# A one-layer hybrid decoder step: the next tile's gate chain moved into the current tile, half of a projection and a broadcast moved ahead

## The chip, the cores and the metric

One NeuronCore of a Trainium2 chip runs the program. The metric is the device time of one execution in microseconds (us). TensorE is called PE here, VectorE DVE, ScalarE ACT, GpSimd POOL, and SyncE, which issues the DMAs, SP.

## What is computed

A prompt of 2048 tokens (and 8 sample tokens, one step each) goes through one layer: RMSNorm, one input projection, two attention branches side by side, gates, an output projection, a residual and a final norm.

```python
u = _rmsnorm(h, norm_g)
gla, g_gate, (sq, sk, sv), s_gate = _project(u, w_in, w_gate_up, b_gate)
o_gla, S = _gla_branch(*gla, s0, gla_norm)      # linear attention with a decay per key channel
o_swa, k_new, v_new = swa_fn(sq, sk, sv)        # 128-wide window, softmax with a sink
h = h + _merge(o_gla, g_gate, o_swa, s_gate, w_out)
```

The decay comes from a small gate chain: a low-rank projection `g_low` (16 columns), times `w_gate_up`, plus a bias, gives z; `log_a = log_sigmoid(z) / 16`; its running sums give the factors by which queries and keys of the linear attention are scaled. The outputs are the normed rows, the states and the last keys and values.

## The kernel before

The prompt is cut into 16 tiles of 128 tokens (`NT`). The loop is written out: each engine has its own program, `body(t)` for t = 0 to 14, and a last tile, t = 15, in which the 8 sample tokens (`S`, width 8) take the place of the next tile. Semaphore counts alone tie the engines together. Weights are resident as f16 pairs, high and low part, and every product of the projections is three f16 matmuls (L511, L512, L513: high x high, high x low, low x high).

`body(t)` on PE works on two tiles at once: the attention of tile t, and the projections of tile t + 1 (`nxt`), which fill PE while the other engines work. The projections come in six groups: gqk (queries and keys of the linear attention), sq (window queries), sklow (window keys, values, and the low rank), gv (values of the linear attention), gg and sg (the gates). Before the change the order is: turn_low and gate_up (the low-rank rows of tile t transposed, L628, and multiplied to z, L635) around gqk; scores (L595), sq; turn_probs of softmax units 0 and 1 (L607: transposes), scores of units 2 and 3, sklow; values (the products with the window values) of units 0 and 1; turn_probs of 2 and 3; leaf_scores (L647), the whole of gv, values of 2 and 3 with the level scores (L661) between; turn_keys (L669); a part of gg; gla_out (L681, L685) and state_update (L696); the rest of gg, 5/8 of sg; turn_out (L708), the rest of sg; out_proj half 0, bc(t + 2), out_proj half 1. bc (L521) spreads the reciprocal norms of tile t + 2 over the partitions; DVE makes its diagonal in norm_x (L1245) and uses its result in scale_u (L1251), then ACT and DVE split the normed tile into u_hi and u_lo (L949, L1257), which the projections of the next iteration read.

PSUM banks are handed out in rings: a list of names per tile, taken in turn over two banks, and a name may be written once the name two places before it in the list has been freed by the engine that reads it. The ring of the projections is

```python
pj = Ring(banks[0:2], sem("proj_full"), {"act": sem("proj_freed_act"), "dve": sem("proj_freed_dve")},
          [("bc", "dve"), ("gqk", "act"), ("sq", "act"), ("sklow", "dve"), ("gv", "dve"),
           ("gg", "act"), ("sg", "act")],
```

and `wait_free` says for the first two names of the list (i < 2) which name of the tile before they wait for:

```python
self.wait_freed(eng, self.order[len(self.order) + i - 2][0], t + -1)
```

The gates are read by ACT in take_gate (a Silu, L971), after its take_out (L1041, the copies of the transposed rows) and norm_rows; a table is loaded before the first Silu, and another after the second. The exponentials of the softmax are ACT's L1003, on what DVE's row_max (L1397 to L1404) leaves; probs_hi (L1014) and DVE's take_pt (L1411, L1415) make f16 pairs of the transposed values. The gate chain behind z is: take_z (DVE, L1295, L1298), log_gate (ACT, L981 to L985), sums (DVE, L1304 to L1315 with L405, L406), differences (POOL, L1869), decays (ACT, L989 to L996), factors (DVE, L1322 to L1333). Tile 0 (`early`) has its projections ahead of the loop, amid the weight preparation.

## Time and profile before

| | |
|---|---|
| time, median of 3 runs | 963.75 us (962.51 to 964.22) |
| the profiled execution | 962.79 us, of which the span of its instructions 960.8 |
| busy: PE, weight loads, DVE, ACT, POOL | 889.7, 618.8, 689.4, 399.4, 57.6 us |
| share of the span | 93%, 64%, 72%, 42%, 6% |
| granted clock of PE, mean | 0.957 |
| chain that ended last | PE 73%, DVE 21%, issue 2%, ACT 2%, DMA 1% |

A profile row names line, engine, operation, output and inputs, the number of instructions merged, busy time, and the idle time of the engine just before, with the instruction that ended it. `flex` is one large buffer that holds most of the loop's intermediate values, so its name tells little and the line more. Busy PE is not PE at its peak: matmuls overlap, and their starts tell the pace. In a wait with two conditions the later one decides.

### The profile page before, as it was taken

Reading aid. Unit: us, or ns where it says so; the run is one execution under the profiler, and the core shown is the slowest. Engines: PE = TensorE matmul, PEld = TensorE weight load, DVE = VectorE, ACT = ScalarE, POOL = GpSimd, SP = SyncE. Lnnn points to the kernel's source line nnn. Section 1 sums busy time; section 2 is a strip of 40 time slices with the busy share of each in tenths; the row PEclk is TensorE's granted clock in tenths of the full one; section 3 lists DMA queues with packets and bytes.
Section 4 is the critical chain, followed back from the end, with each engine's and each line's share of the span. In section 5 each row is a group of like instructions: output and inputs, shape, how many; then the busy total and the mean of one; then the engine's idle time right before and its main releaser. Section 6 shows DMA issues by size and latency. Waiting matters only on the chain.

```text
span 960.8 us, 21676 instructions
## 1 busy us (share of the span) xinstructions
PE 889.7 (93%) x8701; PEld 618.8 (64%) x8701; DVE 689.4 (72%) x2140; ACT 399.4 (42%) x1096; POOL 57.6 (6%) x101
## 2 busy tenths in 40 slices
PE   1697699999999999999999999999999999999977
PEld 1673457585857666675758585766767575856755
DVE  5999858586776859495867678594959585776673
ACT  6885434343534243343434342434434343433311
POOL 0000101010101001010101010000101010101000
PEclk9798699999999999999999999999999999997776
DMA  9640102020202010010202020201102020101220
GB/s 381 249 166 0 67 1 89 1 90 1 89 1 89 2 66 24 23 67 2 89 1 90 1 89 2 89 1 42 49 4 86 1 89 1 48 2 45 78 113 24
DMA packets 15219, 56.47 MB, mean 59 GB/s; under 512 B 3569, under 2 KB 5001, under 8 KB 13840
## 3 DMA queue, kind: packets, MB, share of 16 engines
q1 hardware_dynamic: 14832, 55.02, 15.3%
q8 instruction: 69, 1.13, 0.5%
q14 instruction: 30, 0.25, 0.1%
q10 hardware_dynamic: 288, 0.07, 0.0%
HBM read 44.30 MB, written 10.78 MB: 57 GB/s over the span
## 4 chain that ended last, share of the span: by engine, by line
PE 73%; DVE 21%; issue 2%; ACT 2%; DMA 1%; SPq 0%; DVEq 0%
PE bank L511 19%; PE bank L512 19%; PE bank L513 19%; DVE flex L1404 4%; PE bank L661 3%; DVE bank L1398 2%; PE bank L595 2%; DVE flex L406 2%; PE bank L708 2%; PE bank L685 1%; PE bank L681 1%; DMA w_out_lo<-in_w 1%; DVE flex L1309 1%; PE bank L647 1%; DVE flex L405 1%
## 5 line engine op out<-in xcount | busy, mean ns | idle before, releaser
L511 PE MATMUL bank<-u_hi,w_in_hi_lo 128*128 128x128 f16 (+1 forms) x1288 | 208.8, 215 | 12.6 <-DVE w_in_hi_lo L1546 12.3
L512 PE MATMUL bank<-u_lo,w_in_hi_lo 128*128 128x128 f16 (+1 forms) x1288 | 208.4, 215 | 0.0
L513 PE MATMUL bank<-u_hi,w_in_hi_lo 128*128 128x128 f16 (+1 forms) x1288 | 208.4, 215 | 0.0
L511 PE MATMUL bank<-w_in_hi_lo,u_hi 128*128 128x512 f16 (+3 forms) x528 | 177.2, 344 | 0.8 <-issue 0.6
L512 PE MATMUL bank<-w_in_hi_lo,u_hi 128*128 128x512 f16 (+3 forms) x528 | 176.9, 343 | 0.0
L513 PE MATMUL bank<-w_in_hi_lo,u_lo 128*128 128x512 f16 (+3 forms) x528 | 176.8, 343 | 0.0
L511 PEld LDWEIGHTS bank<-u_hi,w_in_hi_lo 128*128 128x128 f16 x1288 | 124.2, 99 | 24.7 <-DVE w_in_hi_lo L1546 12.5
L512 PEld LDWEIGHTS bank<-u_lo,w_in_hi_lo 128*128 128x128 f16 x1288 | 124.2, 99 | 0.2
L513 PEld LDWEIGHTS bank<-u_hi,w_in_hi_lo 128*128 128x128 f16 x1288 | 124.2, 99 | 0.0
L511 PE MATMUL bank<-w_out_hi,ogT_hi 128*128 128x512 f16 x256 | 98.0, 383 | 0.0
L512 PE MATMUL bank<-w_out_lo,ogT_hi 128*128 128x512 f16 x256 | 97.9, 382 | 0.0
L513 PE MATMUL bank<-w_out_hi,ogT_lo 128*128 128x512 f16 x256 | 97.8, 382 | 0.0
L513 PEld LDWEIGHTS bank<-w_in_hi_lo,u_lo 128*128 128x128 f16 (+1 forms) x528 | 52.1, 99 | 46.8 <-issue 0.8
L511 PEld LDWEIGHTS bank<-w_in_hi_lo,u_hi 128*128 128x128 f16 (+1 forms) x528 | 52.2, 99 | 44.8 <-issue 4.7
L512 PEld LDWEIGHTS bank<-w_in_hi_lo,u_hi 128*128 128x128 f16 (+1 forms) x528 | 52.1, 99 | 39.2 <-issue 0.6
L1251 DVE TENSOR_TENSOR xT<-xT,bank 128x1024 f32<-128x1024 f32 (+1 forms) x17 | 19.7, 1162 | 78.8 <-PE bank L521 78.8
L1003 ACT ACTIVATE flex<-flex,win_stat 128x128 f32<-128x128 f32 x128 | 50.3, 394 | 23.8 <-DVE win_stat L1404 23.8
L1041 ACT CAST ogT_hi<-bank 128x512 f16<-128x512 f32 x32 | 17.3, 588 | 91.8 <-PE bank L708 91.8
L1869 POOL TENSOR_TENSOR flex<-decay_sum_leaf 128x256 f32<-128x256 f32 x16 | 11.5, 717 | 646.7 <-DVE decay_sum_leaf L1310 646.7
L513 PEld LDWEIGHTS bank<-w_out_hi,ogT_lo 128*128 128x128 f16 x256 | 25.3, 99 | 30.8 <-issue 1.1
L511 PEld LDWEIGHTS bank<-w_out_hi,ogT_hi 128*128 128x128 f16 x256 | 25.4, 99 | 29.9 <-issue 3.8
L512 PEld LDWEIGHTS bank<-w_out_lo,ogT_hi 128*128 128x128 f16 x256 | 25.2, 99 | 28.1 <-issue 0.8
(263 smaller groups left out, 1765.3 us busy)
## 6 DMA issues: line engine op xcount, KB each, us to landing
xT<-in_xT SPq DMA_DIRECT2D x16, 512.0 KB, 4.5
x_rows<-in_xq SPq DMA_DIRECT2D x16, 512.0 KB
flex<-in_w SPq DMA_DIRECT2D x4, 2048.0 KB, 9.9
flex<-in_xq SPq DMA_DIRECT2D x16, 512.0 KB, 3.5
out_y<-flex SPq DMA_DIRECT2D x16, 512.0 KB, 2.6
w_out_lo<-in_w SPq DMA_DIRECT2D x2, 2048.0 KB, 9.9
w_out_hi<-in_w SPq DMA_DIRECT2D x1, 2048.0 KB, 10.2
w_out_hi<-in_w SPq DMA_DIRECT2D x1, 1088.0 KB, 7.2
```

The costliest lines, as they stand in the source:

```text
L406: return E.tensor_tensor(o[:, :, s:2 * s], b[:, :, s:2 * s], mid, ALU.subtract)
L511: nc.tensor.matmul(out, a_hi, b_hi, start=start and i == 0, stop=False)
L512: nc.tensor.matmul(out, a_hi, b_lo, start=False, stop=False)
L513: mm = nc.tensor.matmul(out, a_lo, b_hi, start=False, stop=stop and i == last)
L595: mm = nc.tensor.matmul(at_ring.bank(name, t)[:, i * 2 * P:(i + 1) * 2 * P], sq[r:r + HD, t.p, 2 * pair + i, :], kwin[r:r + HD, t.p, :], s ...
L661: mm = nc.tensor.matmul(bank[:, c:c + P], EX[:, l0 + l, f, :], QE[:, l0 + l, f].rearrange("p h c -> p (h c)"), start=True, stop=True)
L708: tp = nc.tensor.transpose(bank[:, k * P:k * P + n], gates[0:n, c:c + P], ident[0:n, 0:n])
L1003: e = nc.scalar.activation(PR[:, u % 2, i, :], PR[:, u % 2, i, :], ACT.Exp, scale=-1.0, bias=wst[:, 0, k:k + 1], accum_out=wst[:, 1, k:k + 1])
L1041: nc.scalar.copy(ogT_hi[:, 4 * g:4 * g + 4, 0:n], bank[:, :, 0:n]).then_inc(act_o.sem, 1)
L1251: V.tensor_tensor(xT[:, :, 0:n], xT[:, :, 0:n], bcast(pj.bank("bc", t)[:, 0:n], 1, DT), ALU.mult).then_inc(pj.freed["dve"], 1)
L1398: V.copy_predicated(bank[:, :, P:2 * P], bcast(older[:, :].bitcast(I32), 1, 2), bank[:, :, 0:P]).then_inc(dve_w.sem, 1)
L1404: m = V.tensor_tensor_reduce(PR[:, u % 2, i, :], bank[:, i, P:2 * P], band[:, first], -1.0, nsink[:, k:k + 1], ALU.add, ALU.min, wst[:, 0, ...
```

## The change

The order of the work changes, not the work. The gate chain of tile t + 1 runs at the end of tile t: turn_low and gate_up stand around the first part of gg on PE, take_low and log_gate around head_norm on ACT, take_z after take_gv on DVE, sums after norm_x, factors between residual and final_norm, decays after take_gate, differences behind gates_over_sums on POOL. split_v moves behind sums. The first four of eight steps of gv stand ahead of the first values, the rest where gv stood. bc(t + 2) stands ahead of both halves of the output product. The last tile loses its own chain; tile 0 gets one of its own in the bank accS, which is free there. The turn ring's list is reordered, the last tile has a list without the two gate names, and KST moves to another part of `flex`.

```diff
@@ -117,12 +117,15 @@
 
-    def __init__(self, banks, full, freed, order, tail=None, head=None):
+    def __init__(self, banks, full, freed, order, tail=None, head=None, last=None):
         self.banks, self.full, self.freed, self.order = banks, full, freed, order
+        self.last = order if last is None else last
         self.tail = order if tail is None else tail
         self.head = [(u, n) for n in range(2) for u, _ in order] if head is None else head
 
     def _list(self, t):
+        if t.static and t.off == NT - 1:
...
         QL = part(FT * P).rearrange("p (f c) -> p f c", f=FT)
         AT = part(HG * P).rearrange("p (h c) -> p h c", h=HG)
         assert at[0] <= 8192
         lsum = sb("decay_sum_leaf", [P, FT, P])
         ogT_hi = sb("ogT_hi", [P, DT, P], F16)
@@ -306,8 +309,14 @@
                         ("leaf0", "dve"), ("leaf1", "dve"), ("L1", "dve"), ("L2", "dve"),
                         ("y0", "dve"), ("y1", "dve")])
         tr = Ring(banks[4:6], sem("turn_full"), {"act": sem("turn_freed_act"), "dve": sem("turn_freed_dve")},
-                  [("glT", "act"), ("z", "dve"), ("pt0", "dve"), ("pt1", "dve"), ("pt2", "dve"), ("pt3", "dve"),
-                   ("KST", "act"), ("SU", "dve"), ("og0", "dve"), ("og1", "dve")])
+                  [("pt0", "dve"), ("pt1", "dve"), ("pt2", "dve"), ("pt3", "dve"), ("KST", "act"),
+                   ("glT", "act"), ("z", "dve"), ("SU", "dve"), ("og0", "dve"), ("og1", "dve")],
+                  last=[("pt0", "dve"), ("pt1", "dve"), ("pt2", "dve"), ("pt3", "dve"), ("KST", "act"),
+                        ("SU", "dve"), ("og0", "dve"), ("og1", "dve")])
...
             def turn_low(t):
+
                 tr.wait_free(pe, "glT", t)
-                pj.wait_freed(pe, "sklow", t)
-                nc.tensor.transpose(tr.bank("glT", t)[0:RANK, 0:P], glow[:, t.p, :], ident[:, :]).then_inc(tr.full, 1)
+                pj.wait_freed(pe, "sklow", t + 1)
+                nc.tensor.transpose(tr.bank("glT", t)[0:RANK, 0:P], glow[:, 1 - t.p, :], ident[:, :]
+                                    ).then_inc(tr.full, 1)
 
...
+            def first_turn_low():
+                pj.wait_freed(pe, "sklow", Tile(0))
+                nc.tensor.transpose(accS[0:RANK, 0:P], glow[:, 0, :], ident[:, :]).then_inc(low_turned, 1)
+
+            def first_gate_up():
+                pe.wait_ge(low_taken, 1)
+                for f in range(FT):
+                    mm = nc.tensor.matmul(accS[:, (f + 1) * P:(f + 2) * P], wgu[:, f * P:f * P + P], glT[:, :],
+                                          start=True, stop=True)
+                mm.then_inc(z_full, 1)
...
@@ -836,9 +862,7 @@
                 nxt = t + 1
                 early = t.static and t.off == 0
                 if not early:
-                    turn_low(t)
                     proj(nxt, "gqk")
-                    gate_up(t)
                     scores(t, 0)
                     proj(nxt, "sq")
                 turn_probs(t, 0)
@@ -846,6 +870,7 @@
                 scores(t, 1)
                 if not early:
                     proj(nxt, "sklow")
+                    proj(nxt, "gv", 4)
                 values(t, 0)
                 values(t, 1)
                 turn_probs(t, 2)
@@ -856,16 +881,18 @@
                 if early:
                     proj_rest(nxt, "gg", 3, 6)
                 else:
-                    proj(nxt, "gv")
+                    proj_rest(nxt, "gv", 4)
                 values(t, 2)
                 level_scores(t, "L1", 0)
                 values(t, 3)
                 level_scores(t, "L2", 2)
                 turn_keys(t)
+                turn_low(t)
                 if early:
                     proj_rest(nxt, "gg", 6)
                 else:
                     proj(nxt, "gg", 3)
+                gate_up(t)
                 gla_out(t)
                 state_update(t)
                 if not early:
@@ -874,16 +901,14 @@
                 turn_out(t, 0)
                 turn_out(t, 1)
                 proj_rest(nxt, "sg", 5)
-                out_proj(t, 0)
                 if not (t.static and t.off + 2 > NT):
                     bc(t + 2)
+                out_proj(t, 0)
                 out_proj(t, 1)
...
             t = Tile(NT - 1)
-            turn_low(t)
             proj(S, "gqk")
-            gate_up(t)
             scores(t, 0)
...
             def body(t):
                 nxt = t + 1
                 early = t.static and t.off == 0
-                if not early:
-                    take_low(t)
+                if early:
+                    log_gate(t)
+                else:
                     take_qk(nxt)
-                log_gate(t)
                 probs(t, 0)
                 probs(t, 1)
...
-                decays(t)
+                if early:
+                    decays(t)
                 probs(t, 2)
                 probs(t, 3)
                 probs_hi(t, 2)
                 probs_hi(t, 3)
                 sink_term(t)
                 take_kst(t)
+                take_low(t)
                 if not (t.static and t.off + 2 > NT):
                     square_rows(t + 2)
                 head_norm(t)
+                log_gate(nxt)
                 take_out(t, 0)
                 take_out(t, 1)
                 if not (t.static and t.off + 2 > NT):
@@ -1181,21 +1217,19 @@
                 take_gate(nxt, 0)
                 take_gate(nxt, 1)
                 nc.scalar.preload_act_table_set(LOG_EXP_SET)
+                decays(nxt)
                 if not (t.static and t.off + 2 > NT):
                     split_u(t + 2)
                 final_norm(t)
 
...
@@ -1768,18 +1812,18 @@
             def body(t):
                 nxt = t + 1
                 early = t.static and t.off == 0
-                if not early:
-                    take_z(t)
+                if early:
+                    sums(t)
+                else:
                     row_max(t, 0)
                     row_max(t, 1)
-                sums(t)
                 take_pt(t, 0)
                 take_pt(t, 1)
                 row_max(t, 2)
                 row_max(t, 3)
                 if early:
                     dve.wait_ge(init, 2)
-                factors(t)
+                    factors(t)
                 take_pt(t, 2)
                 if not early:
                     take_kv(nxt)
@@ -1789,7 +1833,7 @@
                 assemble_levels(t)
                 if not early:
                     take_gv(nxt)
-                    split_v(nxt)
+                take_z(t)
                 if not (t.static and t.off + 2 > NT):
                     mean_square(t + 2)
                 gate_window(t)
...
                     norm_x(t + 2)
+                sums(nxt)
+                if not early:
+                    split_v(nxt)
                 if not (t.static and t.off + 2 > NT):
                     scale_u(t + 2)
                     split_u(t + 2)
                 residual(t)
+                factors(nxt)
                 final_norm(t)
...
             def body(t):
-                differences(t)
                 gates_over_sums(t)
+                differences(t + 1)
 
```

The other functions named `first_...` are twins of take_low and take_z for tile 0, with semaphores of their own.

The order on PE, from tile 1 (L734 is turn_out, L530 the broadcast, which were L708 and L521; the product's three matmuls are L520 to L522, which were L511 to L513; the ring of projections is in banks 0 and 1). Before:

```order
L708 MATMUL bank5<-ident,flex 128x128 [waits dve_out,turn_freed_dve]
L708 MATMUL bank5<-ident,flex 128x128 x3
L511 MATMUL bank0<-w_in_hi_lo,u_hi 128x512
L512 MATMUL bank0<-w_in_hi_lo,u_hi 128x512
L513 MATMUL bank0<-w_in_hi_lo,u_lo 128x512
L511 MATMUL bank2<-w_out_hi,ogT_hi 128x512 [waits turn_freed_dve,attn_freed_dve]
L512 MATMUL bank2<-w_out_lo,ogT_hi 128x512
L513 MATMUL bank2<-w_out_hi,ogT_lo 128x512
...
L521 MATMUL bank1<-rstd_diag,ones 128x128 [waits dve_norm,proj_freed_act]
L511 MATMUL bank3<-w_out_hi,ogT_hi 128x512 [waits attn_freed_dve]
```

After the change:

```order
L734 MATMUL bank5<-ident,flex 128x128 [waits dve_out,turn_freed_dve]
L734 MATMUL bank5<-ident,flex 128x128 x3
...
L520 MATMUL bank0<-w_in_hi_lo,u_hi 128x512
L521 MATMUL bank0<-w_in_hi_lo,u_hi 128x512
L522 MATMUL bank0<-w_in_hi_lo,u_lo 128x512
L530 MATMUL bank1<-rstd_diag,ones 128x128 [waits dve_norm,proj_freed_act]
L520 MATMUL bank2<-w_out_hi,ogT_hi 128x512 [waits turn_freed_dve,attn_freed_dve]
```

The broadcast of tile 3 stood behind the 24 matmuls of the first half of the output product, and now stands ahead of them, behind nine matmuls of sg; its two waits, on DVE's norm and on ACT's freed count, are the same.

What frees its bank: ACT's rows of the same place after the change, take_out to take_gate (L1074, L965, L967, L996; bank1 is the bank of gg there, and of the broadcast above):

```order
L1014 ACTIVATE flex<-flex 128x256 [waits turn_freed_dve]
L1016 ACTIVATE flex<-flex 128x256 [waits act_gla]
L1018 ACTIVATE flex<-flex 128x256 [waits act_gla]
L1074 CAST ogT_hi<-bank4 128x512 [waits turn_full]
L1074 CAST ogT_hi<-bank5 128x512 [waits turn_full]
L965 ACTIVATE x_stat<-x_stat 128x1 [waits dve_norm]
L967 ACTIVATE x_stat<-x_stat 128x1 [waits act_norm]
L996 ACT_TABLE_LOAD [waits turn_full]
L996 ACTIVATE flex<-bank1,inv_scale 128x512 [waits proj_full]
L996 ACTIVATE flex<-bank0,inv_scale 128x512 [waits proj_full]
L1219 ACT_TABLE_LOAD
```

The order of these rows is that of before; log_gate of the next tile now stands ahead of the two copies.

On DVE behind the diagonal, before (L1245 the diagonal, L1251 and L1257 the normed tile, L1487 residual):

```order
L1245 TENSOR_SCALAR rstd_diag<-ident,x_stat 128x128 [waits proj_full,dve_norm]
L1251 TENSOR_TENSOR xT<-xT,bank1 128x1024 [waits proj_full,xT_in]
L1257 TENSOR_TENSOR u_lo<-xT,u_hi 128x1024 [waits act_norm]
L1487 SCALAR_TENSOR_TENSOR flex<-bank2,row_unscale,flex 128x512 [waits attn_full,dve_out,xres_in]
L1487 SCALAR_TENSOR_TENSOR flex<-bank3,row_unscale,flex 128x512 [waits attn_full]
```

After the change (L1279 the diagonal, L1348 to L1359 sums, L1311 to L1317 split_v, L1285 and L1291 the normed tile):

```order
L1279 TENSOR_SCALAR rstd_diag<-ident,x_stat 128x128 [waits proj_full,dve_norm]
L1348 TENSOR_TENSOR flex<-flex 128x256 [waits dve_gla,act_gla]
L1350 TENSOR_SCALAR flex<-flex 128x256 [waits dve_gla]
L1353 SCALAR_TENSOR_TENSOR flex<-leaf_scan,flex 128x128 [waits dve_gla]
...
L1359 TENSOR_TENSOR flex<-flex 128x256
L1311 CAST win_v_hi_lo<-win_v 128x128 [waits proj_freed_dve]
L1312 TENSOR_TENSOR win_v_step<-win_v 128x128
...
L1285 TENSOR_TENSOR xT<-xT,bank1 128x1024 [waits proj_full,xT_in]
L1291 TENSOR_TENSOR u_lo<-xT,u_hi 128x1024 [waits act_norm]
L1531 SCALAR_TENSOR_TENSOR flex<-bank2,row_unscale,flex 128x512 [waits attn_full,dve_out,xres_in]
L1531 SCALAR_TENSOR_TENSOR flex<-bank3,row_unscale,flex 128x512 [waits attn_full]
```

Sums and split_v now stand between the diagonal and the normed tile.

## Rows read from the trace of the kernel before

**Rows 1.** Busy by stretch: length, PE, PEld, DVE, ACT, POOL, granted clock, DMA, GB/s.

```profile
420.12:472.41 52.29, 51.57 (x493) 35.51 (x494) 37.38 (x120) 20.78 (x60) 3.56 (x6) 1.00 0.11 42
120.00:140.00 20.00, 17.64 (x95) 8.78 (x96) 10.34 (x28) 7.79 (x19) 0.00 (x0) 1.00 0.00 1
```

**Rows 2.** Waits, PE alone, whole run: engine line <- releaser: us, times, longest.

```profile
PE bank L607 <- ACT flex L1003: 17.1, 17, 5.3
```

**Rows 3.** PE timeline, mid tile: start us, us, what, count, idle before.

```profile
466.06 0.61 PE L607 MATMUL bank<-ident,flex 128*128 128x128 f32 x4
...
471.28 0.41 PE L607 MATMUL bank<-ident,flex 128*128 128x128 f32 x2
472.41 0.41 PE L607 MATMUL bank<-ident,flex 128*128 128x128 f32 x2 [0.72 <-ACT flex L1003]
```

**Rows 4.** ACT timeline, the last rows of units 1 and 3.

```profile
463.86 0.19 ACT L1003 ACTIVATION_READ_ACCUMULATOR flex<-flex,win_stat 128x1 f32 x1
...
472.08 0.19 ACT L1003 ACTIVATION_READ_ACCUMULATOR flex<-flex,win_stat 128x1 f32 x1
```

**Rows 5.** Waits of the weight loads, 160 to 875 us.

```profile
PEld bank L607 <- issue: 12.1, 13, 0.9
```

**Rows 6.** PE timeline, end of that tile's predecessor, turn_out to turn_low.

```profile
440.03 1.04 PE L708 MATMUL bank<-ident,flex 128*128 128x128 f32 x8
440.90 0.38 PE L511 MATMUL bank<-w_in_hi_lo,u_hi 128*128 128x512 f16 x1
...
442.84 0.38 PE L511 MATMUL bank<-w_out_hi,ogT_hi 128*128 128x512 f16 x1
...
448.02 0.38 PE L521 MATMUL bank<-rstd_diag,ones 128*128 128x128 f32 x2
...
453.42 0.27 PE L628 MATMUL bank<-ident,g_low 128*16 128x128 f32 x1
```

**Rows 7.** ACT timeline, the same place: table load and Silus of take_gate.

```profile
442.09 1.28 ACT L971 ACT_TABLE_LOAD   x1
443.39 1.26 ACT L971 ACTIVATE flex<-bank,inv_scale 128x512 f32<-128x512 f32 x2
```

**Rows 8.** One line, L971: duration ns min/median/max, over the whole run.

```profile
L971 ACT ACTIVATE flex<-bank,inv_scale x32: 678/684/690, 98.1 to 862.3; 128x512 f32<-128x512 f32 x32
```

**Rows 9.** DVE timeline, from the diagonal to the next tile's factors.

```profile
443.06 0.29 DVE L1245 TENSOR_SCALAR rstd_diag<-ident,x_stat 128x128 f32<-128x128 f32 x1
448.52 1.22 DVE L1251 TENSOR_TENSOR xT<-xT,bank 128x1024 f32<-128x1024 f32 x1 [5.17 <-PE bank L521]
...
451.99 0.74 DVE L1487 SCALAR_TENSOR_TENSOR flex<-bank,row_unscale,flex 128x512 f32<-128x512 f32 x1
453.63 0.75 DVE L1487 SCALAR_TENSOR_TENSOR flex<-bank,row_unscale,flex 128x512 f32<-128x512 f32 x1 [0.90 <-PE bank L513]
455.59 0.15 DVE L1494 TENSOR_SCALAR h_stat<-h_stat 128x1 f32<-128x1 f32 x1 [1.22 <-ACT junk L1046]
...
456.83 1.28 DVE L1497 SCALAR_TENSOR_TENSOR flex<-flex,h_stat,norm_f 128x1024 f32<-128x1024 f32 x1
...
460.79 0.15 DVE L1397 COPY win_stat<-neg_sinks 128x1 f32<-128x1 f32 x1
...
463.05 0.42 DVE L1304 TENSOR_TENSOR flex<-flex 128x256 f32<-128x256 f32 x1
...
467.44 0.41 DVE L1411 SCALAR_TENSOR_TENSOR flex<-bank,flex 128x256 f16<-128x256 f32 x1
...
471.27 0.42 DVE L1322 TENSOR_TENSOR flex<-gla_q,flex 128x256 f32<-128x256 f32 x1
...
474.80 1.49 DVE L1333 TENSOR_TENSOR flex<-flex,gla_k 128x1280 f32<-128x1280 f32 x1
```

**Rows 10.** PE timeline: turn_out of tile 0, gate_up of the last tile.

```profile
126.24 1.07 PE L708 MATMUL bank<-ident,flex 128*128 128x128 f32 x8 [2.36 <-DVE flex L1468]
...
875.04 0.81 PE L635 MATMUL bank<-g_lowT,w_gate_up 16*128 16x128 f32 x4 [0.43 <-ACT g_lowT L976]
```

More of the change, by code:

```diff
@@ L125, in _list @@
     def _list(self, t):
+        if t.static and t.off == NT - 1:
+            return self.last
         return self.tail if t.sample else self.order
@@ L825, in _ @@
             proj(Tile(0), "gv")
-            turn_low(Tile(0))
+            first_turn_low()
             proj(Tile(1), "gv")
@@ L830, in _ @@
             pe.wait_ge(init, 1)
-            gate_up(Tile(0))
+            first_gate_up()
             scores(Tile(0), 0)
@@ L1130, in _ @@
                 if i == 6:
-                    take_low(Tile(0))
+                    first_take_low()
                 hi_w(i)
@@ L1189, in _ @@
             t = Tile(NT - 1)
-            take_low(t)
             take_qk(S)
-            log_gate(t)
             probs(t, 0)
@@ L1734, in _ @@
                     dve.wait_ge(w_lo_done, i)
-                    take_z(Tile(0))
+                    first_take_z()
                     row_max(Tile(0), 0)
@@ L1823, in _ @@
             take_gv(S)
-            factors(t)
             take_pt(t, 2)
```

37 lines of the change are left out of this document (28 added, 9 removed).

## The prediction

> **What bounds the kernel now.** I read the busy table by stretch first. One tile of the steady loop takes 52.29 us and TensorE (PE) is busy for 51.57 of them, at a granted clock of 1.00, the 2.4 GHz level; VectorE (DVE) works 37.38 us and ScalarE (ACT) 20.78 [rows 1]. So the loop is a row of matmuls: only a hole in it, or a matmul added or taken away, moves the time. Nothing of the arithmetic changes, so the holes decide. The view of waits, PE alone, names one that repeats: the transposes of the softmax values (L607) wait for the exponentials, 17.1 us in 17 waits [rows 2]; three of them belong to tile 0, fourteen to the tiles behind it.
>
> The PE timeline shows the hole of one tile. The transposes of unit 2 start at 471.28 and those of unit 3 at 472.41. Four such transposes in a row occupy 0.43 us (466.06 to about 466.49, as the eight of 440.03 take until 440.90, 0.109 us each), so unit 2 is through at 471.50, and PE stands for 0.92 us [rows 3, 6]. ACT's last row for unit 3 ends at 472.08 + 0.19 = 472.27 [rows 4], so PE follows an ACT end by 0.14 us. The queue of weight loads says the same over 13 tiles: 12.1 us, 0.93 each [rows 5].
>
> **The change, part by part.**
>
> *A. Half of the next tile's value projection (12 matmuls of 512 columns) goes ahead of the first value products.* From 440.90 to 442.84 nine such matmuls take 1.94 us, 0.2156 each [rows 6], so twelve put 2.59 us between the scores and the transposes of units 2 and 3, against a hole of 0.93. It closes in all 14 tiles that have it (tiles 1 to 14; tile 0 keeps its order): 14 x 0.93 = **-13.0 us**. What the twelve leave behind, PE meets later in the same tile, so they cost nothing. Bounds: 0 (if the exponentials came 2.6 us later) and -13.0; DVE reaches row_max of unit 2 earlier, since sums leaves the stretch ahead of it, so I take the whole.
>
> *B. The broadcast of the rstd row (bc, L521) goes from between the two halves of the output product to ahead of both.* Before, it issued at 448.02; its new place is where the output product starts, 442.84, which is 1.94 us behind the last turn_out transpose [rows 6]. It needs two things. The diagonal: DVE ends it at 443.06 + 0.29 = 443.35 [rows 9]. And its bank: bc of tile t+2 takes the PSUM bank in which the gate gg of tile t+1 lies, by the order list of the projection ring, and that bank is free when ACT has finished the first Silu of take_gate. ACT cannot begin it early: take_gate waits for the same turn_out transposes, stands behind the two copies of take_out and the two steps of norm_rows and then loads a table, 442.09 to 443.37 [rows 7]. The first of the two Silus starts at 443.39 and takes 0.684 [rows 7, 8]: 444.07. With the 0.14 us from above bc can start at 444.21, and PE, at that place at 442.84, stands for 1.37 us; everything behind it in PE's queue, the whole output product, waits too. Before, bc came 5.2 us later and both were long done. Log_gate of the next tile, new ahead of take_out on ACT, ends before the transposes (three short activations in a gap in which ACT waits for PE now), so the chain keeps its length. Tile 0 has the same distances: it starts with the transposes at 126.24 [rows 10]. 15 x 1.36 = **+20.4 us**. Bounds per tile: 0 if both are there, 443.35 + 0.14 - 442.84 = 0.65 if only the diagonal holds it, 1.4 by the bank; I take the bank, since the order of the change shows the wait on ACT's freed count.
>
> *C. The gate chain of the next tile (turn_low, gate_up, take_low, take_z, log_gate, sums, decays, factors, differences) goes into this tile.* On PE it is the same instructions: 0.11 + 0.43 us are added to tile 0 and taken from the last tile, where gate_up costs 0.81 and 0.43 of waiting [rows 10]. Around z: PE has 1.94 us of the gate projection between turn_low and gate_up, and ACT's copy of the low-rank rows fits in. DVE takes z, three short instructions, where the five of split_v stood, so by my estimate its chain from gla_out to turn_out keeps its length. On DVE behind the diagonal: sums, 463.05 to 467.44 = 4.4, then split_v, which I put at 1.1, then the xT product to the next step, 448.52 to 451.99 = 3.5 [rows 9]: 443.35 + 9.0 = 452.4, while PE, with the hole of B, asks for u_lo at about 454.7. This is idle time now: DVE waits 5.17 us for bc there [rows 9]. Behind the second residual DVE now has factors, 471.27 to 474.80 + 1.49 = 5.0, ahead of the final norm, 455.59 to 458.11 = 2.5 [rows 9]. Counted from the end of the output product (453.42 before, and the residual starts 0.2 later and takes 0.75), row_max of unit 0 can start at 0.95 + 5.0 + 2.5 = 8.45; it starts at 460.79 - 453.42 = 7.4 before [rows 6, 9]. Unit 1's last row on ACT ends at 464.05, 3.26 behind row_max's start [rows 4, 9], so at 8.45 + 3.26 + 0.14 = 11.85; PE wants that pair at 466.06 + 0.22 - 453.42 = 12.86, less the 0.11 + 0.6 that left this stretch: 12.15 [rows 3, 6]. Margin 0.3 us: no stall, but little room. Tile 0 +0.5, last tile -1.3, of which I give back 0.6, because there the two projections ahead of the transposes have 8 columns and cover less: **-0.2 us**. Bounds -1 to +3.
>
> *D. The rest* (the rings' lists, the buffer moved to another column, the first tile's own semaphores): no instruction is added, 0. The weight load into a group of 64 rows leaves small gaps, and gate_up now has another neighbour: at most 0.1 us per tile either way, +-1.4.
>
> Sum: -13.0 + 20.4 - 0.2 = **+7.2 us**. The profiled execution took 962.79 us, for a span of 960.8 and 2.0 around it, so it would take 970.0; it lies 0.96 under the median of the runs, 963.75, and on that the forecast is **971.0 us**.
>
> A rule that gives another sum: the issue of matmuls in rows is 0.2156 us for 512 columns at full clock. By the Trainium skill (TensorE: Matmul & The Clock Gate, Back-to-back issue gap), matmuls of 512 columns with their weight loads sustain about 131 ns each. The trace disagrees, and the rows decide; by that rule bc would be reached 0.76 us earlier and the sum would be near +18.6.
>
> **The rivals.**
>
> 1. *The bank is no obstacle* (the count that PE waits for is reached in time). Then A stands alone: -13.0 - 0.2, 950.5 us, faster. It decides at 0.87 us per tile: with a shorter hole at bc than that (14 x 0.93 + 0.2 over 15), the change wins. For it: the broadcast waited for nothing where it was. Against it: ACT's rows, with a table load inside the chain. Chance 0.11.
>
> 2. *A partial wait* (the diagonal, or a bank freed half a microsecond sooner): 0.65 to 0.9 per tile, 9.8 to 13.5 against 13.2: 960.4 to 964. Chance 0.10.
>
> 3. *DVE comes late for the next tile's row_max.* The 0.3 us of margin in C is gone if factors and final norm take longer together (the final norm has two round trips to ACT). Each 0.5 us beyond it costs 14 x 0.5 = 7: about 978. Chance 0.10.
>
> 4. *The new hole lets the clock fall.* For it: any hole is idle time of PE. Against it: PE waited 2.36 us ahead of the transposes at 126.24 [rows 10], and from 120 to 140 the granted clock was 1.00, the 2.4 GHz level [rows 1]; the hole here is 1.4. If a stretch of 5 us of work per tile ran at half speed: 15 x 5 = 75, about 1045 us. The Trainium skill (TensorE: Matmul & The Clock Gate, A second HAM failure mode) warns that short, frequent idling between groups of matmuls can make the clock fall and return again and again; by that rule this rival would be what happens, and the row speaks against it. Chance 0.02.
>
> **How the numbers follow.** Main case 0.67, with its own range 966 to 976 (C, D and 0.1 us per tile in B). With rivals 2 and 3 mostly inside, 959 to 978 should hold 8 in 10; left out are rival 1, rival 4 and the ends. A run of this kernel can be told from no change at about 0.2%, 1.9 us. Faster: rival 1 and 0.06 of rival 2, 0.17. Same: the other 0.04 of rival 2. Slower: 0.79.
>
> **What would show it.** In the profile after: L607's wait (L616 now) down from 17.1 us to about 7, tile 0's part (the row at 472.41 puts 0.72 to each of the 14 [rows 3]); a new repeating wait of PE at the broadcast (now L530), 15 times 1.2 to 1.4 us, released by ACT's Silu (now L996); DVE's wait for the broadcast ahead of the xT product, 5 us per tile now, gone; a tile of 52.7 us. If the broadcast waits under 0.9 us, or DVE is named as its releaser, step B is wrong; if the transposes of units 0 and 1 wait, C is.

## The result and the profile after

The changed kernel takes **971.68 us** (median of 4 runs, 970.73 to 973.71) against 963.52 us (962.51 to 964.22) for the kernel before: a ratio of **1.0092, 95% interval 1.0078 to 1.0106**, so slower by 8.2 us. 971.0 us was predicted, in a range of 959 to 978.

The profiled execution has a span of 971.5 us against 960.8; it is the slowest of the four, 2.0 us over the median. The waits of PE, whole run (us in total, times, longest), beside [rows 2]:

```profile
PE bank L530 <- ACT flex L996: 15.6, 14, 1.1
...
PE bank L734 <- DVE flex L1512: 7.9, 2, 5.6
PE bank L616 <- ACT flex L1036: 7.6, 5, 5.2
```

The wait at the transposes of the softmax values (now L616) fell from 17.1 us in 17 waits to 7.6 in 5, and what is left belongs to the first and last tile. A new one repeats 14 times: PE at the broadcast (now L530), released by ACT's Silu (now L996). Its place in one tile, on PE's timeline (start, length, what, count, idle before), which answers to [rows 6]:

```profile
448.28 0.38 PE L522 MATMUL bank<-w_in_hi_lo,u_lo 128*128 128x512 f16 x1
449.78 0.49 PE L530 MATMUL bank<-rstd_diag,ones 128*128 128x128 f32 x2 [1.12 <-ACT flex L996]
450.11 0.38 PE L520 MATMUL bank<-w_out_hi,ogT_hi 128*128 128x512 f16 x1
```

The last gate matmul issues at 448.28, so the next could at 448.50, and the broadcast comes at 449.78: a hole of 1.28 us. It then holds PE until 450.11, 0.33 us, where it took 0.22 in front of other work. On ACT's and DVE's timelines stands who was late, as [rows 7] and [rows 9] had it before:

```profile
447.75 1.28 ACT L996 ACT_TABLE_LOAD   x1
449.04 1.26 ACT L996 ACTIVATE flex<-bank,inv_scale 128x512 f32<-128x512 f32 x2
```

```profile
448.72 0.29 DVE L1279 TENSOR_SCALAR rstd_diag<-ident,x_stat 128x128 f32<-128x128 f32 x1
...
501.62 0.29 DVE L1279 TENSOR_SCALAR rstd_diag<-ident,x_stat 128x128 f32<-128x128 f32 x1
```

The diagonal was there at 449.01. The first Silu, begun at 449.04 behind the table load, ends 0.684 later [rows 8], at 449.72, and PE starts 0.06 behind that. The second pair of DVE rows is the clock I use below: the diagonal is made once per tile, at the same place of the tile, so the distance between two of its rows is the tile's **period**. It is 52.90 us here. Before, the row at 443.06 [rows 9] has its next one at 495.35: 52.29. In every kernel below the period repeats from tile 2 on within 0.03 us (the last one is up to 0.05 shorter), so it separates effects of 0.1 us per tile, which the medians can't.

By stretch, the columns of [rows 1]; the first line is one tile, the other two lie in tile 0:

```profile
449.78:502.68 52.90, 51.78 (x493) 35.29 (x494) 37.52 (x120) 20.81 (x60) 3.56 (x6) 1.00 0.11 41
125.00:130.00 5.00, 2.65 (x12) 1.79 (x11) 3.58 (x11) 1.19 (x3) 0.00 (x0) 0.79 0.00 2
130.00:135.00 5.00, 4.95 (x21) 2.14 (x20) 4.78 (x15) 4.87 (x9) 1.37 (x3) 0.87 0.00 0
```

**Where the 10.7 us of span lie.** The diagonal's first row in the loop is at 131.19 instead of 129.30, the second at 184.45 instead of 181.59, the fifteenth at 871.88 instead of 861.36. So 7.7 us came in the thirteen periods between the second row and the fifteenth, 2.9 in front of them, and 0.2 behind. The 2.9 are not the change's alone: experiment 2, whose program is the same as the kernel before's up to there, has its first row at 130.66, 1.4 later than the kernel before, so executions scatter by that much in this part. What is left of the 2.9, about 1.5, falls together with the first tile's own gate chain and a lower clock in tile 0 (last section); no run parts the two.

### The profile page after: what moved, and what is told of

Its sections match the earlier page's. It is cut to its first block, busy times and chain, and to the rows that moved or that the text cites. A ratio compares the mean times of both kernels' runs of the same rounds, so it can differ in the third digit from the quotient of the medians.

```text
span 971.5 us, 21674 instructions
## 1 busy us (share of the span) xinstructions
PE 893.7 (92%) x8701; PEld 616.5 (63%) x8701; DVE 691.4 (71%) x2140; ACT 399.8 (41%) x1096; POOL 57.5 (6%) x101
## 4 chain that ended last, share of the span: by engine, by line
PE 84%; DVE 7%; ACT 6%; issue 1%; DMA 1%; SPq 0%; DVEq 0%
PE bank L520 22%; PE bank L521 22%; PE bank L522 22%; PE bank L604 3%; PE bank L687 3%; ACT L996 2%; PE bank L707 2%; ACT ogT_hi L1074 2%; PE bank L616 2%; PE bank L711 1%; DMA w_out_lo<-in_w 1%; PE bank L673 1%; ACT flex L996 1%; PE bank L734 1%; PE bank L650 1%
## 5 line engine op out<-in xcount | busy, mean ns | idle before, releaser
L520 PE MATMUL bank<-u_hi,w_in_hi_lo 128*128 128x128 f16 (+1 forms) x1288 | 209.9, 216 | 13.2 <-DVE w_in_hi_lo L1590 12.3
L521 PE MATMUL bank<-u_lo,w_in_hi_lo 128*128 128x128 f16 (+1 forms) x1288 | 209.6, 216 | 0.0
L522 PE MATMUL bank<-u_hi,w_in_hi_lo 128*128 128x128 f16 (+1 forms) x1288 | 209.5, 216 | 0.0
L520 PE MATMUL bank<-w_in_hi_lo,u_hi 128*128 128x512 f16 (+3 forms) x528 | 177.2, 345 | 0.8 <-issue 0.7
L521 PE MATMUL bank<-w_in_hi_lo,u_hi 128*128 128x512 f16 (+3 forms) x528 | 177.3, 344 | 0.0
L522 PE MATMUL bank<-w_in_hi_lo,u_lo 128*128 128x512 f16 (+3 forms) x528 | 176.9, 343 | 0.0
L520 PEld LDWEIGHTS bank<-u_hi,w_in_hi_lo 128*128 128x128 f16 x1288 | 124.3, 99 | 24.9 <-DVE w_in_hi_lo L1590 12.4
L521 PEld LDWEIGHTS bank<-u_lo,w_in_hi_lo 128*128 128x128 f16 x1288 | 124.1, 98 | 1.8
L522 PEld LDWEIGHTS bank<-u_hi,w_in_hi_lo 128*128 128x128 f16 x1288 | 124.2, 99 | 0.0
L520 PE MATMUL bank<-w_out_hi,ogT_hi 128*128 128x512 f16 x256 | 97.9, 382 | 0.0
L521 PE MATMUL bank<-w_out_lo,ogT_hi 128*128 128x512 f16 x256 | 97.9, 382 | 0.0
L522 PE MATMUL bank<-w_out_hi,ogT_lo 128*128 128x512 f16 x256 | 97.7, 382 | 0.0
L1455 DVE SCALAR_TENSOR_TENSOR flex<-bank,flex 128x256 f16<-128x256 f32 x64 | 26.9, 420 | 92.0 <-ACT flex L1047 92.0
L522 PEld LDWEIGHTS bank<-w_in_hi_lo,u_lo 128*128 128x128 f16 (+1 forms) x528 | 52.1, 99 | 47.3 <-issue 1.6
L520 PEld LDWEIGHTS bank<-w_in_hi_lo,u_hi 128*128 128x128 f16 (+1 forms) x528 | 52.2, 99 | 44.3 <-issue 5.8
L521 PEld LDWEIGHTS bank<-w_in_hi_lo,u_hi 128*128 128x128 f16 (+1 forms) x528 | 52.1, 99 | 37.8 <-issue 0.9
L1079 ACT ACTIVATE junk<-flex 128x1024 bf16<-128x1024 f32 x16 | 16.9, 1057 | 77.5 <-DVE flex L1531 77.5
L1074 ACT CAST ogT_hi<-bank 128x512 f16<-128x512 f32 x32 | 17.4, 588 | 74.3 <-PE bank L734 74.3
L1531 DVE SCALAR_TENSOR_TENSOR flex<-bank,row_unscale,flex 128x512 f32<-128x512 f32 x32 | 23.9, 748 | 33.6 <-PE bank L522 33.6
L1925 POOL TENSOR_TENSOR flex<-flex,win_stat 128x512 f32<-128x512 f32 x16 | 16.7, 1042 | 484.7 <-DVE win_stat L1469 484.7
L522 PEld LDWEIGHTS bank<-w_out_hi,ogT_lo 128*128 128x128 f16 x256 | 25.1, 98 | 30.7 <-issue 0.8
```

Of the source, the lines that this page charges most:

```text
L520: nc.tensor.matmul(out, a_hi, b_hi, start=start and i == 0, stop=False)
L521: nc.tensor.matmul(out, a_hi, b_lo, start=False, stop=False)
L522: mm = nc.tensor.matmul(out, a_lo, b_hi, start=False, stop=stop and i == last)
L1074: nc.scalar.copy(ogT_hi[:, 4 * g:4 * g + 4, 0:n], bank[:, :, 0:n]).then_inc(act_o.sem, 1)
L1455: V.scalar_tensor_tensor(out=PT[:, u % 2, 0, 1], in0=tr.bank(f"pt{u}", t)[:, 0:2 * P].rearrange("p (h c) -> p h c", h=2), scalar=P_TOP, in ...
L1531: V.scalar_tensor_tensor(out=x, in0=at_ring.bank(f"y{g}", t)[0:n, :], scalar=isc[0:n, g:g + 1], in1=x, op0=ALU.mult, op1=ALU.add).then_inc ...
```

## The experiments

All ran as timed comparisons with the kernel before on the same chip. A is the split value projection, B the earlier broadcast, C the moved gate chain; 14 tiles take part in A, 14 or 15 in B.

| kernel | parts | us | before, same series | ratio (95% interval) | period, us |
|---|---|---|---|---|---|
| before | none | | | 1 | 52.29 |
| the change | A, B, C | 971.68 | 963.52 | 1.0092 (1.0078 to 1.0106) | 52.90 |
| e1_bc_back | A, C | 950.77 | 962.67 | 0.9883 (0.9869 to 0.9898) | 51.52 |
| e2_split_alone | A | 961.09 | 962.67 | 0.9983 (0.9973 to 0.9992) | 52.23 |
| e3_bc_alone | B | 984.43 | 962.67 | 1.0226 (1.0211 to 1.0242) | 53.68 |
| e4_other_bank | A, B in a free bank, C | 962.62 | 962.67 | 0.9998 (0.9988 to 1.0007) | 52.18 |
| e5_gv_whole | B, C | 984.18 | 964.15 | 1.0212 (1.0197 to 1.0227) | 53.71 |
| e7_chain_alone | C | 963.81 | 964.15 | 1.0001 (0.9991 to 1.0010) | 52.32 |
| e6a_bc_after_1 | A, C, B 3 matmuls later | 962.59 | 964.15 | 0.9985 (0.9976 to 0.9995) | 52.25 |
| e6b_bc_after_3 | A, C, B 9 matmuls later | 951.77 | 964.15 | 0.9873 (0.9859 to 0.9888) | 51.52 |
| e8_dve_later_1 | A, C, DVE 0.34 later | 951.59 | 963.10 | 0.9878 (0.9864 to 0.9893) | 51.52 |
| e9_dve_later_2 | A, C, DVE 0.54 later | 954.60 | 963.10 | 0.9906 (0.9889 to 0.9922) | 51.60 |

**1. The broadcast put back.**

```diff
-                if not (t.static and t.off + 2 > NT):
-                    bc(t + 2)
                 out_proj(t, 0)
+                if not (t.static and t.off + 2 > NT):
+                    bc(t + 2)
                 out_proj(t, 1)
```

> The change with one edit undone: the broadcast of the rstd row stands between the two halves of the output product again; the split value projection and the moved gate chain stay. Theory (the hole in front of the early broadcast is the whole loss, and the split gains what the old hole cost): PE's new wait at the broadcast goes, 14 tiles x 1.2 to 1.3 us, and the time falls from 971.7 to about 951 to 954 us, below the kernel before by 10 to 12. Rival (the loss lies with the gate chain: turn_low and gate_up in their new neighbourhood, or DVE late for the next tile's row_max with factors ahead of it): the wait at the broadcast goes, but the time stays at 960 us or above, and waits at the transposes or in front of gate_up grow.

Measured 950.77 us, 0.9883 of before, just under the expected 951 to 954 and faster than both kernels. The wait at L530 is gone but for the one in the start phase, and no other took its place:

```profile
core 0: us, PE busy (x) PEld busy (x) DVE busy (x) ACT busy (x) POOL busy (x), PEclk, DMA share, GB/s
389.52:441.04 51.52, 51.52 (x494) 35.41 (x493) 37.56 (x119) 20.81 (x60) 3.56 (x6) 1.00 0.12 42
```

PE is busy for the whole of the tile, 51.52 of 51.52 us: no wait is left in it that this view can show. (Small gaps between issues do not show here: in experiment 10 PE is again busy throughout, and the tile is 0.08 us longer.) The period falls by 1.38 us against the change, which is the 1.28 of the hole and the 0.11 by which the broadcast takes longer behind it. The theory stands, and A and C together are worth 0.77 us per tile.

**2. The split alone.**

```diff
                     proj(nxt, "sklow")
+                    proj(nxt, "gv", 4)
                 values(t, 0)
...
                 else:
-                    proj(nxt, "gv")
+                    proj_rest(nxt, "gv", 4)
```

> The kernel before with the split value projection alone (four of the eight contraction steps of gv ahead of the first value products). Theory: the 0.93 us hole in front of the transposes of units 2 and 3 closes in 14 tiles and nothing else moves: 963.5 - 13 = 950.5 us (bounds 949.5 to 952). Rival (the hole moves to the transposes of units 0 and 1, or to the value products, because DVE and ACT are as late as before): a gain of under 8 us, 956 or more, with a new PE wait of 0.3 us or more per tile. A difference between this run and the one with the broadcast put back prices the moved gate chain by itself; I forecast 0 to +3 us for that.

A miss: 961.09 us, 0.9983, and the period falls by 0.06 us where 0.93 was expected. The rival was right in size (956 or more, a new wait of over 0.3 us per tile), but not in place: the wait is neither at the transposes of units 0 and 1 nor at the value products. The price of the moved gate chain, which the expectation wanted to read from the difference between this run and the first and put at 0 to +3 us, comes out at -10.3 (950.77 - 961.09). The waits of PE:

```profile
PE bank L661 <- DVE flex L1340: 10.2, 14, 0.7
...
PE bank L607 <- ACT flex L1004: 7.0, 3, 5.3
```

The hole at the transposes closed as forecast, and 14 new waits of 0.7 us stand at the level scores (L661), three steps on. One of them on PE's timeline, and DVE's timeline in that stretch:

```profile
427.62 1.16 PE L661 MATMUL bank<-flex 128*128 128x128 f32 x8 [0.73 <-DVE flex L1340]
```

```profile
419.76 0.34 DVE L1405 CUSTOM_DVE_ANT_0 flex<-bank,band_bf,neg_sinks 128x128 f32<-128x128 f32 x1
...
420.03 0.42 DVE L1323 TENSOR_TENSOR flex<-gla_q,flex 128x256 f32<-128x256 f32 x1
...
423.55 1.49 DVE L1334 TENSOR_TENSOR flex<-flex,gla_k 128x1280 f32<-128x1280 f32 x1
424.96 0.42 DVE L1412 SCALAR_TENSOR_TENSOR flex<-bank,flex 128x256 f16<-128x256 f32 x1
...
427.15 0.75 DVE L1340 TENSOR_TENSOR flex<-bank,leaf_mask 128x256 f32<-128x256 f32 x2
```

Between row_max (ends 420.1) and take_pt (L1412) stands factors, from 420.03 until take_pt begins at 424.96. From row_max to the leaf scores' assembly (L1340) DVE is never idle, so it is the bound of this stretch, whatever PE does earlier; PE's last matmul in front issued at 426.70, so it could go on at 426.73, and it did at 427.62, 0.89 us later. In the version with A and C, factors is elsewhere and DVE has time to spare at the same place (from experiment 1):

```profile
420.39 0.42 DVE L1455 SCALAR_TENSOR_TENSOR flex<-bank,flex 128x256 f16<-128x256 f32 x1 [3.49 <-ACT flex L1047]
...
422.58 0.75 DVE L1383 TENSOR_TENSOR flex<-bank,leaf_mask 128x256 f32<-128x256 f32 x2
```

**3. The broadcast alone moved.** The inverse of the first edit, in the kernel before.

> The kernel before with the broadcast alone moved ahead of both halves of the output product. Theory (PE stands until ACT's first Silu has freed the bank, 1.3 to 1.4 us in 14 or 15 tiles, and nothing gives it back): 963.5 + 18 to 20 = 982 to 984 us, with PE waits at the broadcast released by ACT's Silu. Rival (part of the hole is given back, because the transposes of the next tile's units 2 and 3 come later against an ACT and DVE that did not lose the time): the old wait at the transposes is partly gone, and the time lies at 968 to 978.

984.43 us, 1.0226, 0.4 above the expected 982 to 984; the period grows by 1.39 us.

```profile
PE bank L607 <- ACT flex L1003: 17.1, 17, 5.3
PE bank L521 <- ACT flex L971: 16.8, 15, 1.1
```

The wait at the transposes stands unchanged at 17.1 us, so nothing is given back, and the rival falls.

**4. The broadcast in another bank.**

```diff
+                late = t.static and t.off >= 2
+                if not late:
+                    pj.wait_free(pe, "bc", t)
-                pj.wait_free(pe, "bc", t)
                 dve_u.wait(pe, "diag", t)
-                nc.tensor.matmul(pj.bank("bc", t)[:, 0:n], ...
+                nc.tensor.matmul((accS if late else pj.bank("bc", t))[:, 0:n], ...
...
```

The rest, not shown, turns DVE's read of the broadcast in scale_u to the same bank.

> The change, with the broadcast (from the third tile on) written into the bank of the stick-breaking sums, which is free there, so that it no longer waits for the bank that the gate projection occupies; its place ahead of the output product stays. Theory (the bank is what holds it, the diagonal would hold it half as long): the hole falls from 1.28 to about 0.65 us, 14 x 0.63 = 8.8 us less than the change, about 963 us; the releaser that is named becomes DVE. Rival (the wait is for the diagonal in any case): no difference, 971 to 972.

962.62 us, 0.9998. The period falls by 0.72 us against the change, a little more than the 0.63 expected. The releaser changes as the theory wants:

```profile
445.14 0.49 PE L532 MATMUL bank<-rstd_diag,ones 128*128 128x128 f32 x2 [0.40 <-DVE rstd_diag L1281]
```

PE was free at 444.59, so the diagonal holds it 0.55 us, and the broadcast behind the wait takes the 0.11 more that it takes in the change. So the two conditions of step B are seen apart: the diagonal costs 0.66 us per tile against the version with the broadcast put back (52.18 - 51.52), the bank another 0.72. With the bank free, the change would have been a draw with the kernel before.

**5. Without the split.** A undone in the change, by the second edit in reverse.

> The change with the value projection whole again behind the leaf scores (the early broadcast and the moved gate chain stay). If the split is worth the old hole of 0.93 us in 14 tiles also here: 971.7 + 13 = about 985. But the split alone gave the kernel before only 1.6 us, since the level scores waited for DVE in its place. Theory 1 (split and gate chain work only together: the chain takes DVE's late factors out of the stretch, and without the split the hole at the transposes stays): 982 to 985. Theory 2 (the moved chain alone lets DVE and ACT reach the exponentials of units 2 and 3 earlier, so it already closes most of the hole, and the split adds little): 972 to 976. The wait of PE at the transposes, 0 to 0.9 us per tile, tells them apart.

984.18 us, 1.0212: theory 1. The waits at the transposes are back, 16.2 us in 19 waits, beside 15.7 us at the broadcast:

```profile
PE bank L616 <- ACT flex L1035: 16.2, 19, 5.2
PE bank L530 <- ACT flex L995: 15.7, 14, 1.1
```

**6. The gate chain alone.** The first and the fifth edit together.

> The kernel before with the moved gate chain alone (the value projection whole, the broadcast between the halves of the output product). It completes the table: before 962.7, split alone 961.1, split with chain 950.8. Theory 1 (only together): 961 to 964, with 0.9 us of waiting at the transposes in each tile. Theory 2 (the chain alone opens the room): 951 to 956. What it lies under the run with the value projection whole and the early broadcast is the price of the broadcast again, 20 to 21 us.

963.81 us, 1.0001, theory 1 again, and experiment 5 lies 20.4 us over it, the price of the broadcast as forecast:

```profile
PE bank L616 <- ACT flex L1035: 16.0, 18, 5.2
```

Now the table is whole. In periods: A alone -0.06, C alone +0.03, A and C together -0.77, and B +1.39, +1.39 and +1.38 in the three settings. B simply adds; **A and C pay only together**, because two things end the same stretch: the hole that C leaves open (PE waits for the exponentials) and the one that A leaves open (DVE works on factors). In this trace the hole at the transposes is 0.81 us of the tile:

```profile
419.87 0.42 PE L616 MATMUL bank<-ident,flex 128*128 128x128 f32 x2
420.90 0.41 PE L616 MATMUL bank<-ident,flex 128*128 128x128 f32 x2 [0.62 <-ACT flex L1035]
```

The first two transposes hold PE for 0.22 us, to 420.09, and the next start at 420.90; 52.32 - 51.52 = 0.80 is what A gives on top of C.

Why C alone leaves that hole open stands on DVE's timeline. The first two rows are the kernel before, take_pt of unit 0 and row_max of unit 2, the last two the same in this run:

```profile
467.44 0.41 DVE L1411 SCALAR_TENSOR_TENSOR flex<-bank,flex 128x256 f16<-128x256 f32 x1
...
469.02 0.14 DVE L1397 COPY win_stat<-neg_sinks 128x1 f32<-128x1 f32 x1
```

```profile
415.91 0.42 DVE L1454 SCALAR_TENSOR_TENSOR flex<-bank,flex 128x256 f16<-128x256 f32 x1 [2.51 <-ACT flex L1046]
...
417.50 0.15 DVE L1440 COPY win_stat<-neg_sinks 128x1 f32<-128x1 f32 x1
```

With sums gone from in front of take_pt, DVE stands idle for 2.51 us, because it waits for ACT's probs_hi (L1046). That stands on ACT behind the copy of the window queries (L987), which waited for PE and started at 414.91, just behind sq. Counted from the transposes of units 0 and 1, the next thing behind sq (466.06 before [rows 3], 414.71 here), row_max of unit 2 starts after 2.96 us before and after 2.79 here: 0.17 earlier, not the 4.4 us that sums is long. So taking sums out shortens the way to the exponentials by little, and in experiment 2 I estimate that it would have brought DVE forward by about as much, against a hole of 0.89 us. By these rows it is factors, 5 us long and right behind row_max, whose leaving makes A pay; that is argued from the timelines, and moving factors by itself was not run.

**7 and 8. The broadcast a little later.** The change with the broadcast behind k = 1 and behind k = 3 of the 8 contraction steps of the first half.

```diff
-                    bc(t + 2)
-                out_proj(t, 0)
+                out_proj(t, 0, 0, k)
+                if not (t.static and t.off + 2 > NT):
+                    bc(t + 2)
+                out_proj(t, 0, k, DT)
                 out_proj(t, 1)
```

> The change, with the broadcast behind the first of the eight contraction steps of the output product's first half: three matmuls, 3 x 0.2156 = 0.65 us of cover. Theory (a fixed time at which the bank comes free; PE loses what is left of 1.28 us plus about 0.1 for starting again): hole 0.63 us, 14 x 0.65 = 9 us less than the change, 962.6. Rival (the price is in the order of the queue or in the clock, not in the time that is left to cover): no change from 971.7, or all of it gone at once, 951.

> The change, with the broadcast behind three of the eight contraction steps of the output product's first half: nine matmuls, 1.94 us of cover, more than the hole of 1.28. Theory: no wait at the broadcast, and the same time as with the broadcast between the halves, 950.8 (950 to 952). Rival (splitting a half's accumulation around another matmul has a price of its own, or the wait follows the broadcast): 953 or more.

962.59 and 951.77 us, both on the theory: the periods are 52.25 and 51.52. With one step ahead of it the broadcast costs 0.65 us less per tile, which is the 3 x 0.2156 of the matmuls that now stand in front; with three it costs nothing, as it does between the halves. The wait that is left with one step:

```profile
PE bank L530 <- ACT flex L1000: 6.6, 14, 0.5
```

So it is the time at which the bank comes free that counts, with the matmuls ahead of it as cover. Splitting a half's accumulation around the broadcast shows no price of its own.

**9 and 10. DVE later for the next tile's row_max,** in the version with the broadcast put back.

```diff
                 final_norm(t)
+                V.tensor_copy(AT[:, :, :].rearrange("p h c -> p (h c)"), normf[:, 0:512])
```

The second one adds a copy of 256 columns into another buffer behind it.

> The fastest version so far (the change with the broadcast back between the halves, 950.8 us), with one copy of 512 columns between DVE's final norm and the next tile's row_max, in tiles 1 to 15's stretch ahead of the first exponentials. It adds 0.4 to 0.6 us to DVE there and changes no result. In the trace of that version ACT's last row for unit 1 ends 0.2 to 0.25 us before PE asks for the transposes, less than the 0.3 predicted. Theory (the margin is that thin, and each microsecond beyond it is a hole of PE in every tile): a wait of 0.15 to 0.4 us per tile at the transposes of units 0 and 1, 14 times, so 953 to 957 us. Rival (the margin is wider or the hole is given back at the transposes of units 2 and 3): 951 to 952.

> The same with a second copy, of 256 columns, behind the first: 0.2 to 0.35 us more on DVE. Theory: all of it is lost by PE now that the margin is used up, 14 x 0.2 to 0.35, so 3 to 5 us more than with one copy. Rival: the same time as with one copy.

The first is a miss: 951.59 us and an unchanged period. The copy was shorter than I had put it, and the margin wider. With both copies, DVE's timeline:

```profile
408.08 0.42 DVE L1857 COPY flex<-norm_f 128x512 f32<-128x512 f32 x1
408.42 0.29 DVE L1858 COPY decay_sum_leaf<-norm_f 128x256 f32<-128x256 f32 x1
408.62 0.15 DVE L1441 COPY win_stat<-neg_sinks 128x1 f32<-128x1 f32 x1
```

They push row_max back by 0.34 and 0.20 us. The first costs nothing, the second 0.08 to 0.09 us per tile (51.60 against 51.52). PE's timeline has it at the transposes of units 0 and 1, where step C's margin lies:

```profile
411.74 0.69 PE L616 MATMUL bank<-ident,flex 128*128 128x128 f32 x4
412.36 1.13 PE L604 MATMUL bank<-win_k,win_q 64*128 64x256 f32 x8
```

The four take 0.62 us until the scores start, and 0.53 with one copy (410.87 to 411.40). So the margin is 0.34 + 0.20 - 0.09 = **0.45 us**; behind it, by this one point, PE begins to lose. The tenth run is a miss in its theory too: 0.20 us more on DVE cost 0.09 per tile, about 1.2 us, and not all of it, although the medians are 3.0 us apart, at the edge of the forecast 3 to 5. In the two traces the other part stands behind the last of the diagonal's rows in the loop, 99.26 us with two copies and 96.98 with one. There the clock differs: the granted clock is 0.71 from 863.1 to 873.1 in the one and 0.88 from 859.2 to 869.2 in the other. This stretch lasts from 97.0 to 100.8 us in the twelve traces, so I go by the periods. Whether the second copy has a part in it no run shows.

## Why the prediction was right

**Step A (-13.0 us).** The hole did close in 14 tiles and the exponentials are in time, and nothing appeared behind it. The term measured -0.80 us per tile where 0.93 had been read, 14 x 0.80 = -11.2 us: the stretch of the hole is 0.81 us in the version with C, and 0.91 in the kernel before (472.41 - 471.50). What the step got wrong is what holds PE in this stretch. It said that "what the twelve leave behind, PE meets later in the same tile, so they cost nothing", and asked only whether ACT's exponentials are in time. It never followed DVE up to the next thing that PE takes from it. The rows for that were there: factors, 471.27 to 474.80 [rows 9], stands between row_max and take_pt in the kernel before. Experiment 2 shows the term to be worth 0.06 us per tile without C. Its other reason, that DVE reaches row_max of unit 2 earlier since sums leaves, holds for 0.17 us only (experiment 6). In the sum this did no harm, since C is in the change, and that was luck: the step counted C for the way to the exponentials alone, and what C had to clear was factors, behind them. As a forecast for the split alone, I repeated it and was off by 10 us.

**Step B (+20.4 us).** Right in place, cause and size. The hole was worked out as 1.37 us (the sum then uses 1.36) and is 1.28, since PE followed ACT's end by 0.06 us and not 0.14; the broadcast itself then takes 0.11 more, which the step didn't have, and the period shows 1.38 to 1.39 in three settings. That the size per tile comes out so closely is these two cancelling. In the medians, the change against the version with the broadcast put back is 1.0092 - 0.9883 = 0.0209 of 963.5, 20.1 us. It waited in 14 tiles, not 15. In tile 0 of this execution the clock was at its lower level for a while: five of the nine matmuls in front of the broadcast issued 0.43 us apart instead of 0.22, which covered the hole but for 0.2 us; where the clock stayed up (experiment 3) there are 15 waits. The bounds that the step named, 0.65 by the diagonal alone and 1.4 by the bank, agree with what experiment 4 and the change cost per tile, 0.66 and 1.38; the holes themselves are 0.55 and 1.28.

**Step C (-0.2 us).** The chain alone gives 963.81 against 964.15, a ratio of 1.0001 (0.9991 to 1.0010): nothing, as said. Its two ends, +0.5 in tile 0 and -0.7 in the last tile, were not measured apart. The predicted start of row_max, 8.45 us behind the end of the output product, is 8.22 (468.69 - 460.47):

```profile
468.69 0.14 DVE L1441 COPY win_stat<-neg_sinks 128x1 f32<-128x1 f32 x1
```

The margin, put at 0.3, is 0.45, measured in the version with the broadcast put back. Rival 3, which needed it used up, had a real mechanism, half a microsecond away.

**Step D (0, within 1.4).** C alone is +0.03 us per tile, 0.4 us over 14 tiles.

The terms as measured: 14 x (1.38 - 0.80 + 0.03) = +8.5 us, against the 8.2 us of the medians. Predicted were +20.4, -13.0 and -0.2. In the sum the 1.8 us that A gave less and the 1.1 us that B cost less partly cancel: the forecast of the time is 0.7 us off, that of the difference 1.0 (7.2 against 8.2), its terms up to 1.8. So the closeness of the total is in part luck. The tile of 52.7 us that was to show it is 52.90, mostly by A's 0.13. Of the other signs, the wait at the transposes is down to 7.6 us (about 7 was said), and DVE's wait for the broadcast, 78.8 us in 16 waits before, is gone.

**The rivals.** Rival 1 falls with the releaser named at L530 and with experiment 4 (the limit at which it decides is 13.22 / 15 = 0.88 us per tile, not 0.87, which changes nothing). Rival 2 is what the kernel would have been with a free bank (experiment 4, 962.6, in its span of 960.4 to 964). Rival 4, the clock: in the tile shown above, with its hole of 1.28 us, the granted clock is 1.00, the 2.4 GHz level; so it is over the whole stretch from 185 to 850 us, and from the third on the periods lie within 0.04 us of each other. The Trainium skill (TensorE: Matmul & The Clock Gate, A second HAM failure mode) tells of a kernel in which frequent micro-idling between matmul groups made the clock swing. These repeating holes did not do that here.

The issue rate was the other disputed rule: three matmuls of 512 columns gave 0.65 us of cover in experiment 7, 0.216 each, the rate of [rows 6]. The Trainium skill (TensorE: Matmul & The Clock Gate, Back-to-back issue gap) has about 131 ns as the sustained rate; the runs decide for the rows.

## What to carry to other kernels

Before an instruction is moved forward in a queue that bounds the kernel, look up what it needs at its new place: its data and also the buffer it writes into, whose last reader may sit behind another engine's table load. That the old place shows no wait says nothing of the new one; here, nine matmuls (1.94 us) further back, it was free, and at the front it cost 1.4 us in every tile, more than the rest of the change gained.

Where a hole is closed by more work in front of it, follow every engine through the whole stretch to the next thing that is taken from it: here two engines were late by nearly the same amount (0.91 us at the transposes, 0.89 at the level scores), and removing either lateness alone gained nothing that counts, 0.06 us per tile at most.

## What the runs showed of the hardware that was not expected

**The clock in tile 0 differs between executions of the same code.** Two kernels with the same program up to there, experiments 1 and 9, from 125 to 130 us:

```profile
125.00:130.00 5.00, 2.79 (x11) 2.02 (x12) 3.48 (x10) 1.49 (x5) 0.00 (x0) 0.74 0.00 2
```

```profile
125.00:130.00 5.00, 2.63 (x17) 1.56 (x16) 3.96 (x12) 1.33 (x4) 0.00 (x0) 1.00 0.00 2
```

Both have PE idle for 2.4 us ahead of turn_out's transposes, waiting for DVE; the one fell to the 1.2 GHz level for part of it, the other did not, and the period behind it is 52.86 us in the first and 51.52 in the second. Over all twelve traces this wait is 2.35 to 2.37 us; the granted clock in these 5 us is 0.74 to 0.79 in five (the change, experiments 1, 5, 7, 8) and 1.00 in seven (the kernel before among them). In [rows 10] I had taken this single row as evidence that such a wait doesn't touch the clock; it is one execution's row, and five of twelve have it otherwise. What decides was not tried.

**The broadcast behind a wait holds PE longer, the transposes don't.** The broadcast's two matmuls take 0.33 us until the next starts if PE stood idle in front of them (449.78 to 450.11, and the same in experiments 4 and 7), and 0.22 otherwise (394.49 to 394.71 in experiment 1). There a hole's price is 0.11 us more than the hole. At the transposes it is not: the two behind the wait take 0.34 us until the leaf scores start (472.41 to 472.75 before), and four without a wait 0.56 (427.20 to 427.76 after the change), which is the same 0.34 behind the first two; the hole of 0.81 in experiment 6 cost 0.80. Why the two differ was not tried. And the list of waits shows less than either: 1.12 us per tile for a hole of 1.28 that costs 1.39, so such a row is a lower bound.
